# A PEER layer on one core: sparse path reordered, one-hots from f16 operands in SBUF, U rests on VectorE from block 44 on

## The reference, cut to what matters

```
q = h @ w_q                                   # 8 heads x 256
s1, s2 = q[:128] @ keys1.T, q[128:] @ keys2.T # 8 heads x 128 scores, twice
v1, i1 = top_k(s1, 16); v2, i2 = top_k(s2, 16)
top_v, top_i = top_k(v1[:,None] + v2[None,:], 16)        # 16 of 256
ids = i1[top_i // 16] * 128 + i2[top_i % 16]  # of 16384 experts
w = softmax(top_v)
out = sum_k w_k * gelu(h . u[ids_k]) * v[ids_k]          # 128 picks a token
```

## Time and profile before

| what | us |
| --- | --- |
| runs | 1749.70, 1738.14, 1730.55; median 1738.14 |
| profiled execution, its own time | 1742.43 |
| its span, first to last instruction | 1740.6 |
| PE busy | 1556.9 (89%) |
| DVE busy | 1283.6 (74%) |
| POOL busy | 590.2 (34%) |
| ACT busy | 578.2 (33%) |
| mean granted TensorE clock | 0.956 |
| DMA | 432.58 MB, 249 GB/s over the span |

### The profile page before, as it was taken

One profiled execution on the slowest core, in us unless ns is written; L12 is line 12 of the kernel. 1 busy time (PEld: TensorE's weight loads), 2 busy tenths in 40 slices (PEclk: granted clock), 3 DMA queues, 4 the chain that ended last, 5 costly groups with the idle time before them and its releaser, 6 DMA issues.

```text
span 1740.6 us, 21713 instructions
## 1 busy us (share of the span) xinstructions
PE 1556.9 (89%) x8105; PEld 1346.9 (77%) x8105; DVE 1283.6 (74%) x2203; ACT 578.2 (33%) x842; POOL 590.2 (34%) x405
## 2 busy tenths in 40 slices
PE   5899987959999999779999996737999999999997
PEld 1588776748899999769999986736877888777776
DVE  1675366563299999689999965646888888878785
ACT  3323232332233233334444441202333333333333
POOL 0000000010146665456666677851222222222211
PEclk8899998979999999889999998978999999999999
DMA  8386110303344444368999999998999999999972
GB/s 331 106 314 221 37 49 25 104 6 97 121 144 159 162 165 168 104 216 294 325 322 311 317 345 418 394 401 315 368 345 375 359 369 368 350 356 351 343 288 96
DMA packets 162674, 432.58 MB, mean 249 GB/s; under 512 B 13744, under 2 KB 71472, under 8 KB 161456
## 3 DMA queue, kind: packets, MB, share of 16 engines
q1 hardware_dynamic: 124224, 293.64, 46.8%
q0 software_dynamic: 36864, 134.23, 20.5%
q10 hardware_dynamic: 1520, 3.93, 0.6%
HBM read 377.22 MB, written 54.53 MB: 248 GB/s over the span
## 4 chain that ended last, share of the span: by engine, by line
PE 47%; DMA 14%; POOL 6%; DVE 4%; ACT 3%; issue 3%; SPq 1%; ACTq 0%; DVEq 0%; POOLq 0%
PE ps L1483 15%; PE ps L1485 15%; PE ps L1484 15%; DMA blk_raw<-v_nat 9%; POOL ws_lo L555 5%; DMA rows<-u_nat,ids 3%; PE ps L1808 2%; POOL rows L563 1%; DMA g_dram<-g_buf 1%; ACT ws_hi L861 1%; DVE ps L1446 1%; ACT ws_hi L818 1%; DVE ws_lo L1431 1%; PE ps L1760 1%; DMA w_dram<-w_stage 1%
## 5 line engine op out<-in xcount | busy, mean ns | idle before, releaser
L1483 PE MATMUL ps<-hT_hi,ws_hi 128*128 128x384 f32 (+1 forms) x1184 | 423.7, 358 | 44.4 <-POOL ws_lo L555 43.2
L555 POOL TENSOR_TENSOR ws_lo<-blk_raw,ws_hi 128x1024 fp32r<-128x1024 f32 x128 | 326.8, 2553 | 332.6 <-ACT ws_hi L818 331.1
L1485 PE MATMUL ps<-hT_hi,ws_lo 128*128 128x384 f32 (+1 forms) x1184 | 412.0, 348 | 0.0
L1484 PE MATMUL ps<-hT_lo,ws_hi 128*128 128x384 f32 (+1 forms) x1184 | 411.7, 348 | 0.0
L1483 PE MATMUL ps<-ws_hi,coef_hi 128*128 128x512 f32 x768 | 302.4, 394 | 44.5 <-DVE coef_lo L1434 44.5
L1484 PE MATMUL ps<-ws_lo,coef_hi 128*128 128x512 f32 x768 | 300.5, 391 | 0.0
L1485 PE MATMUL ps<-ws_hi,coef_lo 128*128 128x512 f32 x768 | 300.3, 391 | 0.0
L1483 PEld LDWEIGHTS ps<-hT_hi,ws_hi 128*128 128x128 f32 x1184 | 227.7, 192 | 67.5 <-POOL ws_lo L555 30.6
L563 POOL DMA_INDIRECT rows<-v_nat,ids x128 | 129.1, 1009 | 349.6 <-DVE ps L1446 319.6
L1431 DVE TENSOR_TENSOR ws_lo<-blk_raw,ws_hi 128x1024 fp32r<-128x1024 f32 x128 | 156.7, 1224 | 115.6 <-ACT ws_hi L861 114.2
L861 ACT ACTIVATE ws_hi<-blk_raw 128x1024 fp32r<-128x1024 f32 x128 | 135.9, 1062 | 318.0 <-PE ps L1485 240.4
(11 more groups left out here) (276 smaller groups left out, 1927.4 us busy)
## 6 DMA issues: line engine op xcount, KB each, us to landing
blk_raw<-u_t SPq DMA_DIRECT2D x128, 512.0 KB
blk_raw<-v_nat SPq DMA_DIRECT2D x128, 512.0 KB
g_dram<-g_buf SPq DMA_DIRECT2D x128, 192.0 KB
w_dram<-w_stage SPq DMA_DIRECT2D x48, 512.0 KB
grp_g<-g_dram SPq DMA_DIRECT2D x32, 768.0 KB
grp_w<-w_dram SPq DMA_DIRECT2D x32, 768.0 KB
part_w<-w_ada SPq DMA_DIRECT2D x32, 512.0 KB, 6.1
raw<-w_in SPq DMA_DIRECT2D x20, 512.0 KB, 7.0
```

Of the source, the lines that this page charges most:

```text
L555: pool.tensor_tensor(ws_lo[b % 2][:], blk_raw[b % U_RING][:], ws_hi[b % 2][:].bitcast(F32), ALU.subtract).then_inc(u_lo, 1)
L1483: pe.matmul(o, lh, rh, start=start, stop=False, skip_group_check=True)
L1484: pe.matmul(o, lh, rl, start=False, stop=False, skip_group_check=True)
L1485: return pe.matmul(o, ll, rh, start=False, stop=stop, skip_group_check=True)
```

## The change: what it does

- The spreads begin at block 42 and end ahead of block 96. ScalarE's exponentials follow block 39 in place of block 53.
- In the query stage VectorE searches the keys of token block 3 pair by pair between its other work (`take_pair`); `top16` works on `s_all` itself and the copy into `s_work` is gone; `eq` lies in PSUM.
- The operands of the one-hots are f16 in SBUF (`picks_h`, `iota_b`), where they were f32 in SBUF and PSUM.
- From block 44 on VectorE makes the rests of `u` (`rest_u`); GpSimd then has gathers alone. Six gathers stand after block 16, four after block 43.
- `act_row`: 4 before block 42, then 1 in a block with a spread and 3 in one without, and 58 over blocks 96 to 119. `mix_row`: 16 in blocks 120 to 127, 112 in the V stage.
- The stores of `g` and the group loads are issued by ScalarE instead of SP; the first three groups after block 122.
- The V stage has four split buffers (`vs_hi`, `vs_lo`) instead of two, and four `coef_hi`, `coef_lo`.

```diff
 STEPS = ND // TOK_STEP
-PART_A = 54
+PART_A = 42
+EXP_AT = PART_A - 3
+REST_DVE = PART_A + 2
...
+V_RING = 4
...
-U_LATE = 12
-ROW_RATE = 1.15
-def rows_at(v):
-    return min(math.floor((v + 1) * ROW_RATE), U_LATE + PICKS) - min(math.floor(v * ROW_RATE), U_LATE + PICKS)
+EARLY_ROWS = 4
+MIX_FROM = 120
+def share(count, i, n):
+    return (i + 1) * count // n - i * count // n
+def act_rows(b):
+    if b < PART_A:
+        return EARLY_ROWS if b == PART_A - 1 else 0
+    if b < PART_END:
+        return 3 if spreads_after(b) is None else 1
+    early = EARLY_ROWS + STEPS + 3 * (PART_END - PART_A - STEPS)
+    return share(PICKS - early, b - PART_END, MIX_FROM - PART_END) if b < MIX_FROM else 0
+def mix_rows(b):
+    if b < MIX_FROM or b >= 2 * EB - 4:
+        return 0
+    if b < EB:
+        return 2
+    late = PICKS - 2 * (EB - MIX_FROM)
+    return share(late, b - EB, EB - 4)
 def gathers_at():
-    placed = [PART_A + 8 * q / 7 for q in range(STEPS)]
-    left = PICKS - U_LATE - len(placed)
-    placed += [PART_END + (EB - PART_END) * k / left for k in range(left)] + [EB] * U_LATE
-    first = [max(13, math.ceil(placed[max(k - G_RING, 0)] + 1.5)) for k in range(PICKS)]
-    return [[k for k in range(PICKS) if first[k] == b] for b in range(EB)]
+    used = [b for b in range(EB) for _ in range(act_rows(b))]
+    first = [max(16, used[k - G_RING] + 2 if k >= G_RING else 0) for k in range(PICKS)]
+    return [[k for k in range(PICKS) if first[k] == b] for b in range(REST_DVE)]
...
-picks_t = at("picks_t", rJ + 4 * K, [3, ND])
-w_round = at("w_round", rJ + 10 * K, [ND], F16)
+w_f32 = at("w_f32", rJ + 4 * K, [ND])
+picks_h = at("picks_h", rJ + 6 * K, [4, ND], F16)
 coef = at("coef", rE + 16 * K, [2, ND])
-coef_hi = at("coef_hi", rE + 20 * K, [2, ND], F32R)
-coef_lo = at("coef_lo", rE + 24 * K, [2, ND], F32R)
+coef_hi = at("coef_hi", rE + 19 * K, [V_RING, ND], F32R)
+coef_lo = at("coef_lo", rE + 25 * K, [V_RING, ND], F32R)
+vs_hi = [at(f"vs_hi{i}", (rE, rE + 8 * K, rA + 16 * K, rA + 24 * K)[i], [D], F32R) for i in range(V_RING)]
+vs_lo = [at(f"vs_lo{i}", (rE, rE + 8 * K, rA + 16 * K, rA + 24 * K)[i] + 4 * K, [D], F32R) for i in range(V_RING)]
...
-w_fine = ps[:, 4, P:P + ND]
-w_coarse = ps[:, 5, 0:ND]
+eq = ps[:, 2:6, :].rearrange("p b n -> p (b n)").rearrange("p (h k a) -> p h k a", h=PH, k=TOPK)
...
-def store_g(b):
-    sp.wait_ge(gelu_done, b + 1)
-    sp.dma_start(g_dram[:, b * ND:(b + 1) * ND], g_buf[:, b % 2, :]).then_inc(g_out[b % 2], 16)
...
-            load_group(g)
     if b + U_RING < EB:
         load_u(b + U_RING)
-    elif b + U_RING - EB < 2:
+    else:
         load_v(b + U_RING - EB)
-    store_g(b)
     q = spreads_after(b)
...
-    if b % GRP == 0 and b // GRP + BUFS - 1 < GROUPS_V:
-        load_group(b // GRP + BUFS - 1)
-    if b == GRP:
+    sp.wait_ge(w_stored[half], 16 * CHUNK_STEPS * (CHUNKS // 2))
+for b in range(U_RING, EB):
+    if b == 3 * U_RING:
         sp.dma_start(x2_back[:], x2_dram.rearrange("(b p) d -> p b d", p=P)).then_inc(x2_in, 16)
-    if b + 2 < EB:
-        load_v(b + 2)
+    load_v(b)
...
 begun = False
-for b, due in enumerate(gathers_at()):
+placed = gathers_at()
+for b, due in enumerate(placed):
     rest(b)
     for k in due:
...
+    act.wait_ge(gelu_done, b + 1)
+    act.dma_start(g_dram[:, b * ND:(b + 1) * ND], g_buf[:, b % 2, :]).then_inc(g_out[b % 2], 16)
+def load_group(g):
+    buf = g % BUFS
+    act.dma_start(grp_g[:, buf, :, :].rearrange("p k n -> p (k n)"),
+                  g_dram[:, g * GRP * ND:(g + 1) * GRP * ND]).then_inc(grp_in[buf], 16)
+    act.dma_start(grp_w[:, buf, :, :, :].rearrange("p a b t -> p a (b t)"),
+                  w_dram[:, :, g * GRP * CHUNK:(g + 1) * GRP * CHUNK].rearrange("a p n -> p a n"),
+                  ).then_inc(grp_in[buf], 16)
 def take_w(q):
...
-    if b == PART_A - 1:
-        act.wait_ge(top_step, TB * per_block)
+    if b == EXP_AT:
+        act.wait_ge(top_step, search_steps)
         act.activation(picks[:, 2, :, :], picks[:, 2, :, :], ACT.Exp).then_inc(exp_done, 1)
     if spreads_after(b) is not None:
         take_w(spreads_after(b))
+    if b == MIX_FROM - 1:
+        act.wait_ge(rows_used, PICKS)
+        act.activation(sp_act[:], sp_act[:], ACT.Gelu).then_inc(sp_gelu, 1)
+    if b == EB - 6:
+        for half in range(2):
+            act.wait_ge(w_stored[half], 16 * CHUNK_STEPS * (CHUNKS // 2))
+        for g in range(BUFS - 1):
+            load_group(g)
 def round_v(b):
     act.wait_ge(blk_in[b % U_RING], 16 * ((EB + b) // U_RING + 1))
     if b < 2:
         act.wait_ge(act_done, EB - 1 + b)
+    elif b < V_RING:
+        act.wait_ge(act_done, EB)
     else:
-        act.wait_ge(v_mm, b - 1)
-    act.activation(ws_hi[b % 2][:], blk_raw[b % U_RING][:], ACT.Copy).then_inc(v_hi, 1)
+        act.wait_ge(v_mm, b - V_RING + 1)
+    act.activation(vs_hi[b % V_RING][:], blk_raw[b % U_RING][:], ACT.Copy).then_inc(v_hi, 1)
     act.wait_ge(coef_done, b + 1)
-    act.activation(coef_hi[:, b % 2, :], coef[:, b % 2, :], ACT.Copy).then_inc(coef_r, 1)
-last_act = min(v for v in range(EB) if sum(rows_at(a) for a in range(v + 1)) >= U_LATE)
+    act.activation(coef_hi[:, b % V_RING, :], coef[:, b % 2, :], ACT.Copy).then_inc(coef_r, 1)
 for b in range(EB):
     round_v(b)
-    if b == last_act:
-        act.wait_ge(rows_used, PICKS)
-        act.activation(sp_act[:], sp_act[:], ACT.Gelu).then_inc(sp_gelu, 1)
+    if b % GRP == 0 and b // GRP + BUFS - 1 < GROUPS_V:
+        if b // GRP + BUFS - 1 == GROUPS_V - 1:
+            for half in range(2):
+                act.wait_ge(g_out[half], 16 * (EB // 2))
+        load_group(b // GRP + BUFS - 1)
...
+def best_keys(tb, hs):
+    top16([s_all[:, tb, (2 * h + a) * KEYS:(2 * h + a + 1) * KEYS] for h, a in hs],
+          [tv[:, a, h, :] for h, a in hs], [ti[:, a, h, :] for h, a in hs], len(hs))
+def take_pair(m):
+    take_s(m)
+    if m % 2:
+        dve.wait_ge(s_taken, m + 1)
+        best_keys(TOP_ORDER[0], [(m // 2, 0), (m // 2, 1)])
+for m in range(2 * PH):
+    if m >= 3:
+        rest_unit(28 + m)
+        take_pair(m - 3)
+for m in range(2 * PH - 3, 2 * PH):
+    take_pair(m)
...
 def search(tb):
-    step(dve.tensor_copy(s_work[:].rearrange("p a h k -> p (a h k)"), s_all[:, tb, :]))
-    hs = [(h, a) for h in range(PH) for a in range(2)]
-    work = s_work[:].rearrange("p a h k -> p (a h) k")
-    top16([work[:, 2 * h + a, :] for h, a in hs], [tv[:, a, h, :] for h, a in hs],
-          [ti[:, a, h, :] for h, a in hs], 2 * PH)
+    if tb != TOP_ORDER[0]:
+        best_keys(tb, [(h, a) for h in range(PH) for a in range(2)])
     step(dve.tensor_tensor(cand[:], tv[:, 0, :, :].unsqueeze(3).broadcast_to([P, PH, TOPK, TOPK]),
                            tv[:, 1, :, :].unsqueeze(2).broadcast_to([P, PH, TOPK, TOPK]), ALU.add))
...
-        step(dve.tensor_tensor(eq[:].rearrange("p h k a -> p (h k) a"),
+        step(dve.tensor_tensor(eq.rearrange("p h k a -> p (h k) a"),
                                cpf[:, half, :].unsqueeze(2).broadcast_to([P, PICKS, TOPK]),
                                iota_k[:].unsqueeze(1).broadcast_to([P, PICKS, TOPK]), ALU.is_equal))
-        step(dve.tensor_tensor(eq[:], eq[:], tif[:, half, :, :].unsqueeze(2).broadcast_to([P, PH, TOPK, TOPK]),
+        step(dve.tensor_tensor(eq, eq, tif[:, half, :, :].unsqueeze(2).broadcast_to([P, PH, TOPK, TOPK]),
                                ALU.mult))
...
-    assert n[0] - before == per_block
     if tb == TD:
         dve.scalar_tensor_tensor(ids[:], picks[:, 0, tb, :], 128.0, picks[:, 1, tb, :], ALU.mult,
                                  ALU.add).then_inc(ids_done, 1)
+assert n[0] == search_steps
+some_rows(EARLY_ROWS)
...
     dve.wait_ge(ptr_done, r + 1)
-    dve.tensor_copy(picks_t[:, r, :], ps[:, 2 + r, 0:ND]).then_inc(ptr_taken, 1)
+    dve.tensor_copy(picks_h[:, r, :], ps[:, 2 + r, 0:ND]).then_inc(ptr_taken, 1)
 dve.wait_ge(ptr_done, 3)
-dve.tensor_scalar(picks_t[:, 2, :], ps[:, 4, 0:ND], W_SCALE, None, ALU.mult).then_inc(ptr_taken, 1)
+dve.tensor_scalar(w_f32[:], ps[:, 4, 0:ND], W_SCALE, None, ALU.mult).then_inc(ptr_taken, 1)
 dve.wait_ge(ptr_taken, 3)
-dve.tensor_copy(w_round[:], picks_t[:, 2, :]).then_inc(ptr_taken, 1)
-dve.tensor_copy(key_row, iota_b[:]).then_inc(key_row_done, 1)
+dve.tensor_copy(picks_h[:, 2, :], w_f32[:]).then_inc(ptr_taken, 1)
 dve.wait_ge(ptr_taken, 4)
-dve.tensor_copy(w_coarse, w_round[:]).then_inc(ptr_taken, 1)
-dve.tensor_tensor(w_fine, picks_t[:, 2, :], w_round[:], ALU.subtract).then_inc(ptr_taken, 1)
-dve.wait_ge(ptr_taken, 6)
-dve.wait_ge(key_row_done, 1)
+dve.tensor_tensor(picks_h[:, 3, :], w_f32[:], picks_h[:, 2, :], ALU.subtract).then_inc(ptr_taken, 1)
+dve.wait_ge(ptr_taken, 5)
 dve.wait_ge(sp_w_done, 1)
-keys_of = key_row.unsqueeze(1).broadcast_to([P, TOK_STEP, P])
+keys_of = iota_b[:].unsqueeze(1).broadcast_to([P, TOK_STEP, P])
 def one_hots(q):
     p = q % 2
-    toks = slice(q * TOK_STEP, (q + 1) * TOK_STEP)
-    def over_keys(row):
```

(73 more changed lines are left out.)

78 lines of the change are left out of this document (27 added, 51 removed).

## The result

The changed kernel takes 1773.46 us, the median of four runs (1773.22 to 1775.61). The kernel before, run beside it, takes 1739.79 (1730.55 to 1749.7). The ratio is 1.0195 with an interval of 1.0138 to 1.0253: slower by about 2%. The profiled execution has a span of 1771.6 us against 1740.6, so 31 us are to be found. They are not in one place.

The account below looks back on a forecast made before the run. Every stage had another limit: PE with VectorE in search and spreads, DMA rate in the tail, PE in the V stage. 675.5 + 12.8 + 351 + 177 + 4 + 529 + 15.6 = 1765, median 1763; range 1745 to 1785.

Parts of the forecast that it names:

- The case named as likeliest: Whole kernel: one-hots stay 1.13 us apart, VectorE alone limits the spreads, bytes set the tail; 1763 us, chance 0.50.
- its deciding step: Spreads, blocks 42 to 95: f16 one-hots stay 1.13 us apart because one operand is a single value read 128 times.
- search ends: Search: fewer copies, first key search moved to the query stage, `eq` product 16 us cheaper; ends at 675.5 us.
- to the one-hots: Between search and one-hots: four early rows, 4.6 us, then 8.2 us as before; one-hots begin at 688.3.
- spreads: Blocks 42 to 95: 192 one-hots, 52 rests and 66 rows on VectorE take 351 us; PE needs less.
- blocks after: Tail, blocks 96 to 127: 70.7 MB at 399 GB/s take 177 us; 4 us more for filling the V stage.
- V stage to the end: V stage with four split buffers and fewer rows a block: 529 us, bounds 522 and 550; then 15.6 us as before.
- the faster one: Spreads: one-hots run at two elements a cycle, about 0.60 us apart; 54 blocks take 280 us, total 1692; chance 0.25.
- the 1 us reserved for its neighbours: Search: 1 us added for slower PSUM access of the instructions next to the `eq` product.
- the no-change rival: Tail runs at PE's pace, 70.7 MB passing in about 145 us, one-hots as forecast; end near 1731; chance 0.12.
- The slower rival: Search: `eq` product keeps 4.35 us in PSUM, search ends 16 us later; 1779, or 1795 with the old V-stage pace; chance 0.13.

Follow-up runs that it names:

- The value pairs: Changed kernel with each token's value stored twice side by side, so every one-hot operand has innermost step 1: 1688.67 us, ratio 0.9725.
- neither: Changed kernel with the rests of u back on GpSimd and the one-hots' operands back to f32 and PSUM: 1732.62 us, ratio 0.9962.
- rests moved: Changed kernel with only the one-hots' operands back to f32 and PSUM, rests staying on VectorE: 1772.33 us, ratio 1.0208.
- operands moved: Changed kernel with only the rests of u back on GpSimd, the one-hots' operands staying f16 in SBUF: 1841.26 us, ratio 1.0603.

## Why the prediction came out as it did

The forecast was 1763 us in a likeliest range of 1745 to 1785; measured were 1773.46. The case named as likeliest is the one that happened, and the experiments carry its deciding step. The forecast was 10 us short. Of these, 7 are in the sum, which gave a span of 1764.9 where 1771.6 were measured. The others came from turning the span into a median: 4.3 us were taken off because the profiled execution before stood above its median, and the one after stood on it. The sum by its terms, against the profiled span:

| term | forecast | measured |
|---|---|---|
| search ends | 675.5 | 684.5 (+9.0) |
| to the one-hots | 12.8 | 15.05 (+2.3) |
| spreads | 351 | 352.5 (+1.5) |
| blocks after | 177 + 4 | 182.8 (+1.8) |
| V stage to the end | 529 + 15.6 | 536.8 (-7.8) |

That the sum is so near is in part luck: terms that were 14.6 us too short met one that was 7.8 too long.

**The one-hots: right, and shown.** I took 1.13 us because the comparison of a repeated value with a row was the nearest row and the copy, the faster one, has a single input. The value pairs bring the distance to 0.60 with the same types and places. Here two rules of the Trainium skill were weighed. "Vector Engine (DVE) Microarchitecture Reference", section "5.1 Performance modes", said that a repeated single element keeps 1x: by that rule 1.13, and the trace has 1.13 to 1.14. Read alone, "VectorE: DVE Perf Modes", section "The perf-mode tier table", gives 2x, and the measurement has that only for the pairs. (The case that the prediction calls the second rival there is the faster one, the first in its list.)

**The spreads: right within 1.5 us.** 192 one-hots, 52 rests and 66 row instructions fill VectorE; the windows show it busy 352.00 of 352. I costed the rests on VectorE and did not ask what f16 operands in SBUF would cost had the rests stayed on GpSimd. The 2 x 2 of the experiments answers it: 1732.6 (neither), 1772.3 (rests moved), 1841.3 (operands moved), 1773.5 (both).

**The search: the step that was mis-sized.** "What makes it slow no row says", I wrote of the product, and bounded the gain by 0 and 16 us. The product did gain 8 x (4352 - 2299) = 16.4 us, but the search gained less, since the cause was a wait behind GpSimd's rest and other instructions met rests instead: comparisons +4.1 us (8 x 0.516), candidate sums +1.8 (4 x 0.455), `ids` +2.2, and the index arithmetic, an instruction with one input, about 1.2 (4 x 0.289). Together 9.3. The sums also began 0.9 us later than forecast (484.64, not 483.75); the product gained 0.4 more than the 16 taken, and the 1 us reserved for its neighbours was not needed as such. That gives 8.8 of the 9.0 us missing. The +2.3 after the search is the same wait in the subtraction of `picks_h` (2.65 us, 0.56 before). Rows could have told it: the earlier trace rows has two instructions of one size at 2.29 and 4.35, and a mean of exactly that excess over all eight asks for the timeline of GpSimd beside it.

**The blocks after the spreads: right, and shown.** I set them by 70.7 MB at 399 GB/s. The time was 182.8 us, at 409 GB/s for 133 us and 351 for the last 49, together about 71.6 MB. The time itself excludes the no-change rival, which had 145 us, and the experiment with 11.5 MB more gave 30 us where its bytes ask for 28. What I placed inside the 177, the stall of a gelu behind the groups' bytes, is a cost of its own: about 8 us came back when the group loads went to SP's queue and earlier.

**The V stage: 8 us better than forecast.** It ran at PE's pace, 524.32 of 527 us busy. 128 blocks at the 4.07 us of the earlier trace rows are 521, and I had taken 529 and 15.6 for the end; the 536.8 measured are 521 and 15.6. The four buffers had no part in it.

**The other cases.** The slower rival (`eq` keeps 4.35 us in PSUM) did not happen; the time nonetheless came within 6 us of its 1779, through the search's waits. The faster one is the pairs kernel, 1692 forecast for it and 1688.67 measured. Its condition was not met in the changed kernel. Its working took the spreads to be set by bytes, 280 us; they took 268 at PE's pace, and the sum agrees only because other terms were short.

## What to carry to other kernels

Before counting on a 16-bit speed-up, look at the innermost step of every operand: a broadcast value has step 0, and storing it as a pair gives the fast form back at the price of a copy that writes twice as much. When two like instructions of one engine differ by a fixed excess, put the timeline of the other engine beside them before pricing a move: here a VectorE instruction with two inputs in SBUF and a rest of GpSimd excluded each other, and moving one tensor out of SBUF took away about half of the waiting, since the rests then met other instructions. Count bytes by stage, and keep loads of megabytes off the queue of stores that someone waits for.

## What the runs showed of the hardware that was not expected

- An f16 one-hot whose repeated value is stored as a pair runs at nearly twice the pace: 0.68 us long, 0.60 apart, against 1.22 and 1.13.
- A rest of 1024 elements on GpSimd, 2.4 us long, mostly holds up the VectorE instruction with two SBUF inputs behind it by 2.05 to 2.2 us, and less where the rest had begun earlier. Some instructions with one input were held up too: index arithmetic from 0.23 to as much as 0.69 us, and once a conversion from 0.29 to 2.46.
- GpSimd's gather instructions for `u` got slower: 1363 ns in the mean, before 952. The group in the changed kernel (shortest, median, longest ns) is below. The cause is open. The median is 1630 here and 1672 with the one-hots' operands back in PSUM, so their place is not it; it is 941 with the value pairs and 953 with rests on GpSimd and a full VectorE. Slow are those with rests on VectorE and a full VectorE. It cost nothing here, since GpSimd has only the gathers left.

```profile
L560 POOL DMA_INDIRECT rows<-u_nat,ids x128: 935/1630/3026, 554.7 to 1162.9; - x128
```

- The fifth of six group-load issues in a row holds ScalarE's queue for 7.61 us, and held SP's for 7.83 before, where the issue in the earlier trace rows takes 0.45.
